# Two transformer blocks on one core: shared expert cut into the routing, a new load order at the start, eight weight slots in the second expert layer

## What is computed

```python
# block 1: 64 experts of hidden width 256, eight per token, and one shared expert
scores = sigmoid(xt @ w_router); eidx = top 8 of (scores + bias) within 4 of 8 groups
y = sum over chosen e of weight * swiglu(xt, w_gate_e[e], w_up_e[e], w_down_e[e])
y = y + swiglu(xt, w_gate_sh, w_up_sh, w_down_sh)
# block 2: 16 experts of hidden width 1024; each expert takes its 32 best tokens
aff = softmax(h @ w_router); gates, idx = top_k(aff.T, 32)
yo = (silu(h[idx] @ w_exp_gate) * (h[idx] @ w_exp_up)) @ w_exp_down * gates
```

## Time and profile before

| | |
|---|---|
| runs, us | 1721.1, 1717.12, 1721.59 (median 1721.1) |
| profiled execution, us | 1716.69 (its span 1714.9) |
| PE busy | 1374.2 us, 80% |
| DVE, ACT busy | 582.4 us, 34%; 440.7 us, 26% |
| HBM over the span | 306 GB/s, 522.53 MB read |
| mean granted PE clock | 0.911 of full |

### The profile page before, as it was taken

How to read it: one execution, slowest core, us unless ns; L and a number is a source line. 1 busy time by engine, 2 the same in 40 slices (tenths; PEclk the granted TensorE clock), 3 DMA queues, 4 the chain that set the end, 5 groups by cost and what they waited for, 6 DMA issues and landing times.

```text
span 1714.9 us, 23335 instructions
## 1 busy us (share of the span) xinstructions
PE 1374.2 (80%) x9178; PEld 876.6 (51%) x9178; DVE 582.4 (34%) x1280; ACT 440.7 (26%) x680; POOL 7.4 (0%) x14
## 2 busy tenths in 40 slices
PE   5999998889998777877779999998856665655665
PEld 4788888764534433432468888997511311212112
DVE  3433666453334223322274665653300100001001
ACT  4433786301111001111053345453200000000002
POOL 0000000000000000000000000000000000000000
PEclk9999999989999889988889999999886878888868
DMA  9777622829999999999944433443599999999995
GB/s 333 268 283 283 234 99 90 320 98 393 413 374 418 399 406 423 405 405 422 387 171 148 147 112 135 177 169 138 205 423 409 422 419 412 422 417 415 422 415 206
DMA packets 123014, 524.62 MB, mean 306 GB/s; under 512 B 9744, under 2 KB 12968, under 8 KB 81472
## 3 DMA queue, kind: packets, MB, share of 16 engines
q1 hardware_dynamic: 121344, 518.68, 76.1%
q0 software_dynamic: 1456, 4.51, 0.9%
q10 hardware_dynamic: 144, 0.44, 0.1%
HBM read 522.53 MB, written 2.63 MB: 306 GB/s over the span
## 4 chain that ended last, share of the span: by engine, by line
PE 55%; DMA 27%; SPq 11%; DVE 3%; issue 2%; ACT 1%; DVEq 0%; ACTq 0%; PEldq 0%
PE psum L1781 21%; DMA ring<-in_w_up_e_dram 11%; DMA ring<-in_w_exp_up_dram 10%; SPq L567 9%; PE psum L2094 9%; DMA ring<-in_w_exp_down_dram 4%; PE psum L2067 3%; PE psum L2139 3%; PE psum L1788 3%; PE psum L2454 2%; DMA ring<-in_w_mem_kv_dram 2%; PE psum L2057 1%; DVE ring_r L997 1%; PE psum L1853 1%; PE psum L1797 1%
## 5 line engine op out<-in xcount | busy, mean ns | idle before, releaser
L1781 PE MATMUL psum<-arena_r,ring_r 128*128 128x256 f32 x3360 | 415.6, 284 | 31.0 <-issue 8.9
L1781 PEld LDWEIGHTS psum<-arena_r,ring_r 128*128 128x128 f32 x3360 | 404.2, 191 | 43.6 <-issue 23.7
L2094 PE MATMUL psum<-ring,arena 128*32 128x512 f32 (+1 forms) x1152 | 188.4, 638 | 78.3 <-DMA ring<-in_w_up_e_dram 77.6
L2454 PE MATMUL psum<-ring,arena 128*32 128x512 f32 x1024 | 160.9, 767 | 90.0 <-DMA ring<-in_w_exp_up_dram 87.4
L997 DVE TENSOR_TENSOR ring_r<-ring,ring_r 128x1024 fp32r<-128x1024 f32 x156 | 181.8, 1220 | 136.7 <-ACT ring_r L647 135.5
L647 ACT ACTIVATE ring_r<-ring 128x1024 fp32r<-128x1024 f32 x156 | 153.2, 1049 | 78.7 <-DMA ring<-in_w_in_dram 35.2
L2094 PEld LDWEIGHTS psum<-ring,arena 128*32 128x32 f32 (+1 forms) x1152 | 56.9, 127 | 193.0 <-issue 186.7
L2472 PE MATMUL psum<-ring,arena 128*32 128x512 f32 x512 | 88.4, 825 | 69.3 <-DMA ring<-in_w_exp_down_dram 66.2
L2454 PEld LDWEIGHTS psum<-ring,arena 128*32 128x32 f32 x1024 | 32.5, 126 | 203.1 <-DMA ring<-in_w_exp_up_dram 138.6
L1724 DVE TENSOR_TENSOR arena<-arena,psum 128x256 f32<-128x256 f32 x16 | 6.7, 421 | 267.1 <-ACT arena L955 267.1
L1387 DVE COPY arena<-psum 128x384 f32<-128x384 f32 (+1 forms) x72 | 42.3, 587 | 152.7 <-PE psum L2067 150.8
(11 more groups left out here) (386 smaller groups left out, 1225.5 us busy)
## 6 DMA issues: line engine op xcount, KB each, us to landing
ring<-in_w_gate_e_dram SPq DMA_DIRECT2D x64, 1024.0 KB, 12.2
ring<-in_w_up_e_dram SPq DMA_DIRECT2D x64, 1024.0 KB, 14.3
ring<-in_w_down_e_dram SPq DMA_DIRECT2D x64, 1024.0 KB, 16.3
ring<-in_w_exp_gate_dram SPq DMA_DIRECT2D x64, 1024.0 KB, 23.4
ring<-in_w_exp_up_dram SPq DMA_DIRECT2D x64, 1024.0 KB, 25.5
ring<-in_w_exp_down_dram SPq DMA_DIRECT2D x128, 512.0 KB, 15.2
ring<-in_w_in_dram SPq DMA_DIRECT2D x20, 2048.0 KB, 8.4
ring<-in_w_ada_dram SPq DMA_DIRECT2D x12, 2048.0 KB, 12.3
```

The costliest lines, as they stand in the source:

```text
L1781: ins = product(lambda a_, b_, k, first, last: mm(ps[:, t * T:(t + 1) * T], a_[:, k, c], b_[:, k, :], start=first, stop=last), w, x, arriving)
L2094: ins = mm(psum[c, 5, :], xg1[:, k, P * j + width * b:P * j + width * (b + 1)], gate[e][:, :, k, :], start=(k == 0), stop=(k == KT - 1))
L2454: ins = mm(psum[32 * q:32 * q + 32, b, :], xg[:, kk, CAP2 * e:CAP2 * (e + 1)], w[:, q // 2, k, (q % 2) * 512:(q % 2 + 1) * 512], start=(kk ...
```

## The change

It has three parts.

**Start.** The order becomes `kkaakaak`. Chunk 0 is loaded ahead of the memory's columns, and its split by ACT and DVE is interleaved with the split of the memory input, quarter by quarter; PE takes the quarters as they come. Both mean squares become one PSUM tile `ms01` of column sums (four groups of 32 rows) after the first half of chunk 0, summed by one matmul `sum01`; one step makes both reciprocal roots. DVE's squares of the memory and the wide `c` move behind the splits. POOL's replication of the bias table waits until `in0_1` is evacuated.

**First expert layer.** The shared expert's gate and up products are cut into eight pieces of four matmuls and put between the sort's steps; `count1`, `tabT` and `eidx` get bank 7 (`PLACED`). DVE's `rows_low` moves between sort steps; the one-hots of the first gather come ahead of the item weights and the integer table; `slot_weights(0)` and the shared product come behind the four gather copies. `w_down_sh` leaves the ring: SP loads it into an arena tile after `table_ready`, and its 16 matmuls stand behind the loop of rounds; the first scatter opens the accumulators.

**Second expert layer.** Two arena tiles of 2 MB are added to the six slots, as third and eighth in an order of eight: the first added one waits for the evacuation of `mO3` (last reader of the memory's keys and values), the second for `mo3`. The first turn stands ahead of a loop of three; its first scatter opens the accumulators and the four zero matmuls go. DVE makes the gather's one-hots ahead of the weighted ones. `row_sums` becomes `column_sums` behind the logits, with a tile `row6` summed from a copy.

```diff
+RING2 = 8
-START = "kaakakak"
+START = "kkaakaak"
...
+PLACED = {"count1": 7, "shu": 1, "start1": 6, "tabT": 7, "itemR": 5, "itemW": 6, "eidx": 7}
...
+        added = [buf(11, SLOT), buf(9, SLOT)]
+        ORDER2 = (0, 1, "first added", 2, 3, 4, 5, "second added")
...
-            sp.dma_start(memT, a["mem_columns"].rearrange("p (k t) -> p k t", t=T)).then_inc(mem_in, 16)
             for n, spec in enumerate(CHUNKS_A):
...
                 if n == 0:
+                    sp.dma_start(memT, a["mem_columns"].rearrange("p (k t) -> p k t", t=T)).then_inc(mem_in, 16)
                     sp.dma_start(xT, a["x_columns"].rearrange("p (k t) -> p k t", t=T)).then_inc(x_in, 16)
...
             sp.wait_ge(table_ready, 1)
+            sp.dma_start(down_sh, a["w_down_sh"][0].rearrange("(k p) c -> p k c", p=P)).then_inc(down_sh_in, 16)
...
                 for c in range(24):
-                    s = (NA + NB + c) % RING
-                    sp.wait_ge(used_b, i * 24 + (NB + c - RING + 1))
+                    place, landed, _ = slot2(c)
+                    if c < RING2:
+                        if ORDER2[c] == "first added":
+                            evacuated(sp, "mO3")
+                        elif ORDER2[c] == "second added":
+                            full(sp, "mo3")
+                        else:
+                            sp.wait_ge(used_b, NB + ORDER2[c] - RING + 1)
+                    sp.wait_ge(used_b, i * 24 + (NB + c - RING2 + 1))
...
             pool.wait_ge(bias_out, 16)
+            evacuated(pool, "in0_1")
...
+            high(0, (0, 1))
             act.wait_ge(mem_in, 16)
-            for k in range(KT):
...
-            high(0)
+            for j in range(4):
...
+                if j < 2:
+                    high(0, (2 + j,))
...
-            for w, nm in enumerate(("itemR", "itemW")):
+            for j in range(1, 4):
+                rows_low(j)
...
+            item_part(0, "itemR")
+            onehots([(0, FULL, 0), (2, FULL, P)])
+            item_part(1, "itemW")
...
-            onehots([(0, FULL, 0), (2, FULL, P)])
-            slot_weights(0, FULL, 0)
             for q in range(4):
                 gather_copy(q, T, 0, q + 1)
+            slot_weights(0, FULL, 0)
+            ps = full(dve, "shu").rearrange("p (k t) -> p k t", t=T)
+            evacuated(dve, "shg")
+            frees(V.tensor_tensor(sha, shg_s, ps, ALU.mult), "shu")
...
+                        ins = V.tensor_scalar(Pg[:, t, c], iota[:, 0:CAP2], items[:, 0, t, bass.ds(i * 4 + j, 1)], None, ALU.is_equal)
+                ins.then_inc(p2_ready, 1)
...
-            project_whole("shg", w[:, 0], hT, 0)
-            project_whole("shu", w[:, 1], hT, 0)
-            full(pe, "shu")
-            used(used_a, 1)
-
+            ps_g = start("shg")
+            for piece in range(3):
+                whole_piece(ps_g, w[:, 0], hT, piece)
             pe.wait_ge(route_ready, 2)
...
+            done(whole_piece(ps_g, w[:, 0], hT, 3), "shg")
+            ps_u = start("shu")
+            whole_piece(ps_u, w[:, 1], hT, 0)
             pe.wait_ge(route_ready, 4)
...
+            whole_piece(ps_u, w[:, 1], hT, 1)
             pe.wait_ge(route_ready, 5)
...
-            wd = chunk_a(n0 + 15, 1024)
+            whole_piece(ps_u, w[:, 1], hT, 2)
+            done(whole_piece(ps_u, w[:, 1], hT, 3), "shu")
...
+            pe.wait_ge(down_sh_in, 16)
+            for m in range(KT):
+                for k in range(2):
+                    mm(acc(m), down_sh[:, k, m * P:(m + 1) * P], sha[:, k, :], start=False, stop=False, skip_group_check=True)
             pe.wait_ge(table_ready, 1)
...
-            row_sums(ps6, sq[0], mo_squares, range(6))
             second_logits(range(6))
+            column_sums(ps6, 0, sq[0], mo_squares, range(6))
...
-            pe.wait_ge(zeros_ready, 1)
...
-            for m in range(0, KT, 2):
-                mm(psum[:, m // 2, :], zeros, cst[:, 0:512], start=True, stop=False, skip_group_check=True)
-            with pe.Fori(0, TURNS2) as i:
...
+            moe2_turn(0, 0)
+            with pe.Fori(0, TURNS2 - 1) as i:
+                moe2_turn(i, 1)
```

More of the change, by code:

```diff
@@ L460, in pieces, with slot2 @@
             return 2 if spec[0] == "shared_gu" or spec[:3] == ("w_in_2", 3072, 512) else 1
+        added = [buf(11, SLOT), buf(9, SLOT)]
+        ORDER2 = (0, 1, "first added", 2, 3, 4, 5, "second added")
+        def slot2(c):
+            j = ORDER2[c % RING2]
+            if j == "first added":
+                return added[0], load_x[0], 0
+            if j == "second added":
+                return added[1], load_x[1], 0
+            s = (NA + NB + j) % RING
+            return ring[:, s, :], load_b[s], sum(pieces(CHUNKS_B[m]) for m in range(len(CHUNKS_B)) if SLOT_B[m] % RING == s)
         def split_views(k, q):
@@ L583, in arrived_moe1, with arrived_moe2 @@
             eng.wait_ge(load_a[s], i + (16 * base + 32 * (m // RING + 1)))
[L585 to L587 removed]
+        def arrived_moe2(eng, i, c, n=0):
+            _, landed, base = slot2(c)
             parts = [2] * 16 + [4] * 8
[L589 to L590 removed]
+            mine = [m for m in range(24) if m % RING2 == c % RING2]
+            once = sum(parts[m] for m in mine)
+            eng.wait_ge(landed, i * (16 * once) + 16 * (base + n * once + sum(parts[m] for m in mine if m <= c)))
         @block.gpsimd
@@ L1040, in scaled @@
                         ins.then_inc(normed, 1)
+            low_part(0, (0, 1))
             dve.wait_ge(mem_in, 16)
-            for j in range(4):
-                squares(memT, sq[0], j)
             mem_hi, mem_lo = PARTS["mem"]
@@ L1267, in _ @@
                 step(V.tensor_scalar(wts[:, e], wts[:, e], den[:, 2 + t:3 + t], 2.5, ALU.mult, ALU.mult))
-            for j in range(4):
-                rows_low(j)
-            ps = full(dve, "shu").rearrange("p (k t) -> p k t", t=T)
-            evacuated(dve, "shg")
-            frees(V.tensor_tensor(sha, shg_s, ps, ALU.mult), "shu")
             ps = full(dve, "rank1")
@@ L1337, in _, with rank_col, weight_col, onehots @@
                 evacuated(dve, nm)
+            def rank_col(t, col):
+                return items[:, 0, t, bass.ds(col, 1)] if not isinstance(col, int) else items[:, 0, t, col:col + 1]
+            def weight_col(t, col):
+                return items[:, 1, t, bass.ds(col, 1)] if not isinstance(col, int) else items[:, 1, t, col:col + 1]
+            def onehots(parts):
+                for col0, kind, c0 in parts:
+                    for t in range(TT):
+                        c = c0
+                        for j, width in kind:
+                            ins = V.tensor_scalar(Pg1[:, t, c:c + width], iota[:, 0:width], rank_col(t, col0 + j), None, ALU.is_equal)
+                            c += width
+                ins.then_inc(pg_ready, 1)
+            item_part(0, "itemR")
+            onehots([(0, FULL, 0), (2, FULL, P)])
+            item_part(1, "itemW")
             ps = full(dve, "eidx")
@@ L1980, in logits, with whole_piece @@
                 done(ins, name)
+            def whole_piece(ps, w, src, piece):
+                t, half = piece // 2, piece % 2
+                for k in range(4 * half, 4 * half + 4):
+                    ins = mm(ps[:, t * T:(t + 1) * T], w[:, k, t * P:(t + 1) * P], src[:, k, :], start=(k == 0), stop=(k == KT - 1))
+                return ins
             def rows_of_h(prefix, after_first):
```

267 lines of the change are left out of this document (139 added, 128 removed).

## The result

The changed kernel takes 1695.1 us (median of 4, 1692.5 to 1695.9), the kernel before 1720.7 on the same chip (median of 4, 1717.1 to 1721.6): a ratio of 0.9856, 95% interval 0.9841 to 0.9871, so 25.6 us off. The profiled execution is the fastest of the four, 1692.54 with a span of 1690.7; the profile shown of before stands at 1716.69 and 1714.9. The two spans differ by 24.2 us. That was forecast as 32.5, to a time of 1686; the range (1675 to 1702) holds the result.

A forecast was written before the change was run, and what follows sets the result against it. PE bounds the dense stages, weight streaming the two expert layers (5.02 us a chunk). Start 9, routing 11.5, second layer 10 and 2 sum to 32.5 off 1716.7 (median 1721.1): 1684.2 to 1688.6, taken as 1686, range 1675 to 1702.

The forecast's parts named there:

- the step that failed: Start, w_in loads near 90 to 120 us: POOL's replication beside them costs 0, or 2 if a split comes late.
- The term of 9: Start: second k chunk's stall, its cold clock and `ms1` go, less new sums and late loads; 9 us, between 3 and 12.7.
- a stall of PE over 3 us in the first 100 us: Start: one of the signs listed as showing the prediction wrong; size over 3 us.
- Routing: First expert layer: pieces fill the sort's pauses, so the first release comes 11.5 us earlier, between 8 and 13.1.
- the ring: Second expert layer: with eight slots, two chunks fewer remain after the first release; 10.0 us gained.
- The earlier release and the cheaper sums: Second layer's first release: 1.1 us from column sums, 0.9 from removing the zero matmuls; together 2 us.
- the third rival: Second layer: both gathers and first weight matmuls cold, or the pause lowers PE's clock; 2.7 worse, 1689; chance 0.08.
- First layer's stream: First expert layer: first release moves the whole stream; `w_down_sh` load costs 0, or 2.5 us without idle DMA time.
- The first: Rival on the start: it gives little, 3 us instead of 9, so 1692; chance 0.12.
- The second: Rival on the second layer: extra slots or earlier release bring half or nothing, 1692 or 1698; chance 0.07.
- The fifth: Rival on the stream into the two added tiles: lower rate makes the kernel slower, 1738 at 374 GB/s; chance 0.03.
- The sixth: Rival on the second layer: a wait in SP's list blocks an added slot's load, six slots in effect, 1696; chance 0.03.

The follow-up runs named there:

- Number 1: Changed kernel with POOL's wait for in0_1 removed, so the bias rows are written as soon as the table is there: 1688.3 us, ratio 0.9809.
- 12: Changed kernel with the bias rows written after the second k chunk's last product is evacuated (wait for memkv1_1 instead of in0_1): 1695.9 us, ratio 0.9866.
- number 7: Changed kernel with the first layer's slot_weights(0) made ahead of the four gather copies, as before the change: 1693.6 us, ratio 0.985.
- Number 3: Changed kernel with all eight shared gate and up pieces together ahead of the sort, down products still behind the loop: 1705.3 us, ratio 0.9904.
- number 4: Changed kernel with six instead of eight slots in the second expert layer, all else of that layer as changed: 1705.1 us, ratio 0.9906.
- number 10: Changed kernel with bias rows written as soon as the table is there and slot weights ahead of the first layer's gather copies: 1685.6 us, ratio 0.9795.
- number 2: Changed kernel with the whole start as before (order kaakakak, bias rows early), routing and second layer as changed: 1690.3 us, ratio 0.9827.
- number 8: Changed kernel without the load of w_down_sh and its 16 matmuls, so the shared expert's output is missing: 1694.5 us, ratio 0.9845.
- number 11: Changed kernel with early bias rows, slot weights ahead of the gather copies, and seven unread matmuls before the second layer's gathers: 1682.2 us, ratio 0.9779.
- number 5: Changed kernel with the bias rows' write cut into four DMAs of two heads, and the reading back into four: 1692.1 us, ratio 0.984.
- 6: Changed kernel with seven unread 512-column matmuls ahead of the second layer's gathers: 1694.2 us, ratio 0.9857.

## Why the prediction was right, and where not

**Start: the step that failed** is "POOL's replication now runs beside the w_in loads near 90 to 120; those have a dozen microseconds of lead", with its price of 0 to 2. That lead was never worked out from rows. Number 1 shows it, where nothing disturbs the loads: a w_in chunk issued at 113.48 is taken by ACT at 121.39 (7.9 us), is split by both engines in about 6 and wanted at 131.36, so the lead is about 4. The write of the rows and the reading back stretch such a load to 17.9: 10 more, less 4 of lead, is a stall near 6 (5.5 measured), and 2.0 follow at the lower clock. What share of the 10 is the write's and what the reading back's was not separated; numbers 1 and 12 move both out of this load. The term of 9 was right as far as it went (8.3 at the first w_in product), and the term beside it, put at 0 to 2, was 7.9 here and up to 11.1 in other profiles. Another 1.3 went by 298 us: 192 matmuls from 273 us end 25.4 us behind their start, where before they needed 23.9, at a mean clock of 0.88 over 270 to 299 against 1.00. The last 0.2 came later. The write's duration, 21.5 us, stood in the earlier trace rows. The test "a stall of PE over 3 us in the first 100 us" looked at the wrong stretch by 35 us. The Trainium skill, "DMA: Bandwidth & Descriptors", section "Issuing engines are not separate DMA queues", says that transfers started by different engines run on the same 16 DMA engines and interleave; the trace agrees, with packets of both queues in flight while the load takes its 17.89 us.

**Routing**: 14.0 against 11.5. The pieces filled the sort's pauses a little better than with the 1.5 us of hand-offs forecast (gathers 20.2 behind instead of 22), and the slot weights cost a wait of 1.68, of which number 7 gives 1.0 back. Number 3 adds what the prediction had not seen: with the down products moved, hardly anything is gained until the pieces fill the pauses; of the pieces' 11.6 us a third (3.9) are steps that take longer at the lower clock.

**Second layer**: the ring was forecast at 10.0 and is 9.6 (number 4). The earlier release and the cheaper sums were forecast at 2 and gave 2.4 in the dense stretch. The other 1.6 of the 11.2 behind the release are no part of the mechanism: the last pass of the stream took 3.38 us before and 1.92 after, 1.5 us of clock level that number 10 loses again. That is luck of the profiles. Both gathers were cold, as the third rival had it, for 3.6 us (7.56 against 1.95 and 2.05 before); its first weight matmuls were not (3.64 for 32, the warm figure). The rule of the Trainium skill that the prediction weighed, "TensorE: Matmul & The Clock Gate", section "Why this matters for your kernels", described the gathers rightly: 3.78 each, and 2.05 with matmuls ahead. That the removal gives nothing did not come out so either, as far as the 2.4 us show: they hold the column sums and the order of the one-hots too, and no run undoes the removal by itself.

**First layer's stream** was taken as unchanged and is 2.4 us longer, in the rounds where a pass of four experts takes 10.01 and 9.47 us instead of 8.48 and 8.71. It isn't the start's (number 2: 485.3), the pieces' (number 3: 485.8) or the down products' (number 8: 485.5). With the slot weights first it was 483.2 (number 7), 484.6 (number 10) and 486.2 (number 11), and 487.1 in number 5, so it isn't the order of the slot weights by itself. The cause stays open.

**Rivals.** The first (the start gives little) had the direction right and the cause wrong: pace and late k loads took little (8.3 of 9 were there at the first w_in product), the bias rows nearly all. The second fell with number 4 (9.6 of the ring's 10). The fifth, slower tiles, fell with turns of 120.6 us; the sixth, a ring of six in effect, with number 4. That the range held is owed in part to errors of both signs: 10.1 and 2.4 lost at the start and in the first layer's stream, 2.5 and 1.6 gained in routing and in the second layer. 32.5 less these 8.4 is 24.1; the difference of the spans is 24.2.

## What to carry to other kernels

When a transfer is moved off one stretch, work out the lead of every load in the stretch that takes it (issue to landing, split, first use) and price the move by the lengthening less that lead; "it runs beside other loads" is no price. Look at both ends of what is moved, the write and the reading back of it. Where one engine's idle pauses are to be filled, move the filler and the cover together: taking a block of work away from a path whose next step waits for another engine can give only a part of its length (here 2.1 of 8.66 us). After a change that gives less than its parts, undo one part at a time: here one line taken back was worth 6.8 us, a quarter of the whole change. And read a stretch in several profiles before pricing it: the start lost 7.9 in one and 11.1 in another of the same kernel.

## What the runs showed of the hardware that was not expected

The write of the bias rows moved 30 GB/s on 0.19 of the DMA engines when two heads were written alone (number 5), and a w_in chunk of 2048 KB beside the end of the whole write and the reading back needed 17.9 us instead of 7.9. The Trainium skill, "DMA: Bandwidth & Descriptors", section "Rules for kernel authors", says that a transfer whose outermost dimension is short runs on few of the 16 engines, and advises to put one of 128 outermost; by it a write of two heads has at most 2 of the 16, a share of 0.13 (an estimate from that rule). The trace agrees for what carries the data: the 24 packets of 4596 bytes in that stretch take a share of 0.11, two of them in flight most of the time; 588 packets of 12 bytes make up the rest of the 0.19. That the shape is why the write is slow, no run here tests. Writing the rows with the 128 copies outermost was not tried and stays open, as does reading the table skewed without a copy at all.

The same scatter at the end of the kernel ran at the lower clock in both profiles with seven unread matmuls 460 us earlier, and in none of the other twelve. Whether the one causes the other isn't shown. The last pass ahead of it ran cold in four profiles (before, 6, 10, 11) and at full clock in the ten others, and the four are those in which at least one of the second layer's first two gathers ran warm.
